# Attention biases with the window masks already in them: shifted tables of 46 rows, border rows loaded in three pieces

## The reference

```python
def row_block(r):
    rs = jnp.clip(r - kr // 2, 0, rows - kr)
    q_r = lax.dynamic_index_in_dim(q, r, axis=1, keepdims=False)
    k_r = lax.dynamic_slice_in_dim(k, rs, kr, axis=1)[:, :, col_idx]
    v_r = lax.dynamic_slice_in_dim(v, rs, kr, axis=1)[:, :, col_idx]
    dr = rs + jnp.arange(kr) - r + (NA_ROW_WIN - 1)
    bias = rpb32[:, dr[None, :, None], dc[:, None, :]]
    sc = jnp.einsum('bqhd,brqwhd->bhqrw', q_r, k_r).astype(jnp.float32) + bias[None]
    p = jax.nn.softmax(sc.reshape(b, NA_HEADS, GRID_W, kr * NA_COL_WIN), axis=-1)
    p = p.reshape(b, NA_HEADS, GRID_W, kr, NA_COL_WIN).astype(v.dtype)
    return jnp.einsum('bhqrw,brqwhd->bqhd', p, v_r)
```

## Time and profile before

| what | us |
|---|---|
| median of 3 runs | 2937.93 |
| lowest and highest run | 2933.5, 2955.96 |
| the profiled execution | 2952.27 |
| its span | 2950.5 |
| TensorE busy in the span | 2737.9 (93%) |
| VectorE busy | 1404.5 (48%) |
| ScalarE busy | 886.3 (30%) |
| POOL busy | 877.5 (30%) |
| input stage | 0 to 655 |
| Fourier stage | 655 to 795 |
| attention | 795 to 1131 |
| mixer output | 1131 to 1520 |
| feed-forward | 1520 to 2950 |

### The profile page before, as it was taken

How to read it: one execution, slowest core, us unless ns; L and a number is a source line. 1 busy time by engine, 2 the same in 40 slices (tenths; PEclk the granted TensorE clock), 3 DMA queues, 4 the chain that set the end, 5 groups by cost and what they waited for, 6 DMA issues and landing times. The chain is left out here.

```text
span 2950.5 us, 33892 instructions
## 1 busy us (share of the span) xinstructions
PE 2737.9 (93%) x12792; PEld 2274.7 (77%) x12792; DVE 1404.5 (48%) x2280; ACT 886.3 (30%) x1595; POOL 877.5 (30%) x491
## 2 busy tenths in 40 slices
PE   7999999998768896999985999997999999999997
PEld 5888888877657785777774888885888888888886
DVE  4300000006458785544336999998565554122232
ACT  3311111112345551211224444443222223343332
POOL 1010011103222224333204666664000004555553
PEclk9999999999879997999997999998999999999999
DMA  4322144426565645555535777776666665564653
GB/s 140 97 93 72 55 133 152 148 96 220 168 155 149 162 125 165 179 186 169 174 107 208 278 280 278 275 285 221 223 221 221 222 221 193 178 204 139 206 175 111
DMA packets 235537, 522.34 MB, mean 177 GB/s; under 512 B 47732, under 2 KB 73200, under 8 KB 231664
## 3 DMA queue, kind: packets, MB, share of 16 engines
q1 hardware_dynamic: 214128, 499.21, 51.3%
q10 hardware_dynamic: 21248, 20.97, 2.1%
HBM read 336.55 MB, written 185.10 MB: 177 GB/s over the span
## 5 line engine op out<-in xcount | busy, mean ns | idle before, releaser
L2205 PE MATMUL ff_psum<-ff_w,ff_hid 128*128 128x512 f32 x2112 | 479.3, 389 | 1.3 <-POOL ff_w L1798 1.3
L2205 PEld LDWEIGHTS ff_psum<-ff_w,ff_hid 128*128 128x128 f32 x2112 | 396.4, 188 | 84.1 <-POOL ff_w L1798 1.7
L1798 POOL TENSOR_TENSOR ff_w<-ff_st,ff_w 128x512 fp32r<-128x512 f32 x176 | 249.5, 1425 | 634.0 <-ACT ff_w L2041 633.6
L1798 POOL TENSOR_TENSOR ff_w<-ff_wraw,ff_w 128x512 fp32r<-128x512 f32 x154 | 269.1, 1749 | 240.9 <-ACT ff_w L2041 240.9
L422 PE MATMUL in_psum<-in_hA,in_w 128*128 128x512 f32 x1440 | 327.9, 389 | 0.0
L422 PEld LDWEIGHTS in_psum<-in_hA,in_w 128*128 128x128 f32 x1440 | 270.4, 188 | 56.0
L2166 PE MATMUL ff_psum<-ff_h,ff_w 128*128 128x512 f32 x1056 | 247.4, 393 | 27.2 <-DVE ff_h L1864 27.2
L2166 PEld LDWEIGHTS ff_psum<-ff_h,ff_w 128*128 128x128 f32 x1056 | 200.5, 190 | 70.6 <-POOL ff_w L1798 28.6
L2166 PE MATMUL ff_psum<-ff_h,ff_again 128*128 128x512 f32 x1056 | 244.7, 391 | 4.0 <-DVE ff_h L1864 4.0
L2166 PEld LDWEIGHTS ff_psum<-ff_h,ff_again 128*128 128x128 f32 x1056 | 199.3, 189 | 45.9 <-issue 4.4
L1464 PE MATMUL mo_psum<-mo_act,mo_w 128*128 128x512 f32 x768 | 191.8, 407 | 33.8 <-POOL mo_act L1315 21.0
(11 more groups left out here) (181 smaller groups left out, 4031.2 us busy)
## 6 DMA issues: line engine op xcount, KB each, us to landing
split<-ff_w SPq DMA_DIRECT2D x154, 512.0 KB, 3.6
ff_again<-split SPq DMA_DIRECT2D x154, 512.0 KB, 4.1
ff_st<-in_w_down_dram SPq DMA_DIRECT2D x176, 256.0 KB, 2.9
ff_wraw<-in_w_up_dram SPq DMA_DIRECT2D x44, 512.0 KB, 5.7
hidden<-ff_c SPq DMA_DIRECT2D x44, 512.0 KB, 3.0
ff_kraw<-hidden SPq DMA_DIRECT2D x44, 512.0 KB, 4.3
at_bias<-shifted SPq DMA_DIRECT2D x72, 256.0 KB
in_raw<-in_w_in_dram SPq DMA_DIRECT2D x32, 512.0 KB, 5.0
```

The lines of the kernel that those rows point to most:

```text
L1798: nc.gpsimd.tensor_tensor(split_out(i, 1), parts(i), f32(split_out(i, 0)), ALU.subtract).then_inc(w_tail, 1)
L2205: last = nc.tensor.matmul(ps[:, 4 * (1 - half) + t], hid[:, a, (b * PAIRS + pair) % 2, q, t * P:(t + 1) * P], weights(i)[:, e], start=(r = ...
```

## The change

Masks are no longer added on chip. They are put into the tables in memory:

- `padded` becomes two tables of 46 rows, filled with -1e30 from a host array. One holds only the 16 columns of offsets that an inner query's window has, the other all 31. Each holds, below one another, a copy with the 8 row offsets of an inner window (the first 31 rows) and one with all 15 (the 15 rows from `NEAR_R`). Four inserts of `rpb` parts for one.
- `shift` goes over 63 pieces for 48: a border query column takes one part of its 32 columns from the full table and the rest from the other. A table has 46 rows for 31, so a shift of full width has 8 x 46 runs of 128 bytes for 8 x 31. They are dealt out evenly over the 48 gate tiles.
- `load_bias` takes row kind 0 and row kind 2 (three column kinds each) in three pieces: one of 3 query rows with 16 key rows (2 KB runs), and for the 5 other query rows two of 8 key rows (1 KB runs). Row kind 1 is loaded as before. That is 21 loads a head for 9, of the same bytes.
- `window`, `sides`, POOL's nine additions, the load of the side masks and VectorE's 72 additions go.
- The reduction waits for the loads of its own row kind (`bias_in[h % 2][i]`) and no more for an addition; the very first tile waits for its own three loads.

```diff
-REL_R, REL_C = 31, 64
+NEAR_R, REL_R, REL_C = 31, 46, 64
+FULL_C = ((0, COL_WIN // 2, 0), (0, 0, 0), (COL_WIN // 2 + 1, QC, COL_WIN))
+SHIFTS = [piece for j in range(KINDS) for c in range(QC)
+          for piece in (((j, c, 0, 0, KC),) if not FULL_C[j][0] <= c < FULL_C[j][1] else
+                        ((j, c, 1, FULL_C[j][2], COL_WIN), (j, c, 0, COL_WIN - FULL_C[j][2], COL_WIN)))]
+ROW_PIECES = (
+    ((0, 3, 0, KR, BASE_R[0] - (QR - 1)), (3, QR, ROW_WIN, KR, BASE_R[0] - (QR - 1)), (3, QR, 0, ROW_WIN, NEAR_R)),
+    ((0, QR, 0, KR, BASE_R[1] - (QR - 1)),),
+    ((3, QR, 0, KR, BASE_R[2] - (QR - 1)), (0, 3, 0, ROW_WIN, BASE_R[2] - (QR - 1)), (0, 3, ROW_WIN, KR, NEAR_R - ROW_WIN)),
+)
...
             def shift(n):
-                j, c = divmod(n, QC)
-                sp.dma_start(shifted[j, :, c], padded[:, :, BASE_C[j] - c:BASE_C[j] - c + KC]
+                j, c, full, k, run = SHIFTS[n]
+                at = BASE_C[j] - c + k
+                sp.dma_start(shifted[j, :, c, :, k:k + run], padded[full, :, :, at:at + run]).then_inc(padded_in, 16)
...
-            sp.wait_ge(zero_done, 1)
+            sp.dma_start(padded.rearrange("f h r c -> (f h r c)").rearrange("(p y) -> p y", p=P), mask).then_inc(padded_in, 16)
...
-                    sp.dma_start(padded[:, PAD_R:PAD_R + RPB_R, PAD_C:PAD_C + RPB_C], rpb).then_inc(padded_in, 16)
+                    for full_c in range(2):
+                        for full_r in range(2):
+                            insert(full_c, full_r)
...
                 for b in range(GB):
-                    shift(GB * t + b)
+                    shifts(GB * t + b)
...
             def load_bias(h, i):
                 for j in range(KINDS):
                     rows = shifted[j, h]
-                    src = bass.AP(rows.tensor, rows.offset + (BASE_R[i] - (QR - 1)) * KC,
-                                  [[KC, QR], [REL_R * KC, QC], [1, KR * KC]])
-                    sp.dma_start(bias[:, h % 2, i * KINDS + j], src).then_inc(
-                        first_in if h == i == 0 else bias_in[h % 2], 16)
+                    for r0, r1, k0, k1, base in ROW_PIECES[i]:
+                        src = bass.AP(rows.tensor, rows.offset + (base + r0 + k0) * KC,
+                                      [[KC, r1 - r0], [REL_R * KC, QC], [1, (k1 - k0) * KC]])
+                        sp.dma_start(bias[r0 * QC:r1 * QC, h % 2, i * KINDS + j, k0 * KC:k1 * KC], src
+                                     ).then_inc(first_in if h == i == j == 0 else bias_in[h % 2][i], 16)
...
-                dve.wait_ge(bias_ready, h * NB + kind + 1)
+                if n == 0:
+                    dve.wait_ge(first_in, 16 * len(ROW_PIECES[0]))
+                else:
+                    loads = KINDS * len(ROW_PIECES[KIND[i]]) * (h // 2 + 1)
+                    if h % 2 == 0 and KIND[i] == 0:
+                        loads -= len(ROW_PIECES[0])
+                    dve.wait_ge(bias_in[h % 2][KIND[i]], 16 * loads)
...
-                b = bias[:, h % 2, kind]
-                V.tensor_tensor(b, b, window[:, kind], ALU.add).then_inc(bias_ready, 1)
```

More of the change, by code:

```diff
@@ L101, with input_phase @@
 RPB_R, RPB_C = 2 * ROW_WIN - 1, 2 * COL_WIN - 1
+FULL_C = ((0, COL_WIN // 2, 0), (0, 0, 0), (COL_WIN // 2 + 1, QC, COL_WIN))
[7 more added lines that the diff above has]
+)
 NEG = -1.0e30
-def input_phase(nc, const_in, step, steps, low, raw, x, w_in, norm_g, b_gate, eye, rpb, u_out, qT_out, v_out, kT_out, gT_out, gate_w,
+def input_phase(nc, const_in, step, steps, low, raw, x, w_in, norm_g, b_gate, eye, rpb, mask, u_out, qT_out, v_out, kT_out, gT_out, gate_w,
                 padded, shifted):
@@ L249, in shift, with insert, shifts @@
             def shift(n):
-                j, c = divmod(n, QC)
-                sp.dma_start(shifted[j, :, c], padded[:, :, BASE_C[j] - c:BASE_C[j] - c + KC]
-                             ).then_inc(padded_in, 16)
-            sp.wait_ge(zero_done, 1)
-            sp.dma_start(padded.rearrange("h r (x c) -> (h r x) c", x=1).rearrange("(p y) c -> p (y c)", y=2),
-                         zero).then_inc(padded_in, 16)
+                j, c, full, k, run = SHIFTS[n]
+                at = BASE_C[j] - c + k
+                sp.dma_start(shifted[j, :, c, :, k:k + run], padded[full, :, :, at:at + run]).then_inc(padded_in, 16)
+            def insert(full_c, full_r):
+                c, nc_ = (0, RPB_C) if full_c else (COL_WIN - 1 - COL_WIN // 2, COL_WIN)
+                r, nr = (0, RPB_R) if full_r else (ROW_WIN - 1 - ROW_WIN // 2, ROW_WIN)
+                at = NEAR_R if full_r else PAD_R + r
+                sp.dma_start(padded[full_c, :, at:at + nr, PAD_C + c:PAD_C + c + nc_], rpb[:, r:r + nr, c:c + nc_]
+                             ).then_inc(padded_in, 16)
+            def shifts(m):
+                slots = NG * GB
+                for i in range(m * len(SHIFTS) // slots, (m + 1) * len(SHIFTS) // slots):
+                    shift(i)
+            sp.dma_start(padded.rearrange("f h r c -> (f h r c)").rearrange("(p y) -> p y", p=P), mask).then_inc(padded_in, 16)
             for q in range(4):
@@ L839, in window_mask, with attention_phase @@
 def window_mask():
[L841 to L858, removed]
+    return np.full((P, 2 * HEADS * REL_R * REL_C // P), NEG, np.float32)
+def attention_phase(nc, const_in, low, raw, qk_in, qT, kT, v, shifted, eye, atT_out):
     KT = KR * KC // P
@@ L887, in attention_phase @@
         ps = m.banks()
-        v_in, bias_in = m.sems("v_in", 2), m.sems("bias_in", 2)
-        sides_in, window_done = m.sem("sides_in"), m.sem("window_done")
+        v_in, bias_in = m.sems("v_in", 2), [m.sems(f"bias_in{i}_", KINDS) for i in range(2)]
         first_in = m.sem("first_in")
-        qk_heads, q_tail, k_tail, bias_ready = (m.sem(x) for x in ("qk_heads", "q_tail", "k_tail", "bias_ready"))
+        qk_heads, q_tail, k_tail = (m.sem(x) for x in ("qk_heads", "q_tail", "k_tail"))
         s_mm, s_red, p_exp, pT_mm, pT_copied, o_mm, inverted, o_done = (
@@ L914, in _ @@
         def _(sp):
-            sp.dma_start(sides[:, 0:KINDS * (KR + KC)], mask).then_inc(sides_in, 16)
             sp.dma_start(ident[:, :], eye).then_inc(const_in, 16)
@@ L972, in _ @@
             G = nc.gpsimd
[L974 to L980, removed]
             up = slice(HEAD_DIM, P)
-            pool.wait_ge(sides_in, 16)
-            window_kind(0, 0)
             for rows, heads in ((slice(0, QR), 3), (slice(QR, ROWS), 2 * PARTS)):
                 pool.wait_ge(qk_heads, heads)
-                pool.wait_ge(window_done, 1 if heads == 3 else KINDS)
+                if heads > 3:
+                    pool.wait_ge(q_tail, 1)
                 G.tensor_tensor(qs[up, 0, rows], qraw[up, rows], f32(qs[up, 0, rows]), ALU.subtract).then_inc(q_tail, 1)
[L989 to L992, removed]
             pool.wait_ge(q_tail, whole(0))
-            for i in range(1, KINDS):
-                for j in range(KINDS):
-                    window_kind(i, j)
             for h in range(1, HEADS):
@@ L2244, in encoder_layer @@
             raw = Pool(nc, ctx, "in").sb("raw", [P, 2 * SEQ])
-            input_phase(nc, const_in, step, steps, low, raw, x, w_in, norm1_g, b_gate, eye, rpb, u, qT, v, kT, gT,
+            input_phase(nc, const_in, step, steps, low, raw, x, w_in, norm1_g, b_gate, eye, rpb, mask, u, qT, v, kT, gT,
                         gate_w, padded, shifted)
             fourier_phase(nc, step, steps, low, raw, qk_in, qT, kT, u, pos_table, chan_table, fnT, gate_w, b_gate, gT)
-            attention_phase(nc, const_in, low, raw, qk_in, qT, kT, v, shifted, mask, eye, atT)
+            attention_phase(nc, const_in, low, raw, qk_in, qT, kT, v, shifted, eye, atT)
         mixer_output_phase(nc, const_in, step, steps, x, fnT, atT, gT, w_mix, w_out, norm2_g, eye, x2, hT)
```

17 lines of the change are left out of this document (4 added, 13 removed).

## The result

The changed kernel takes 2993.2 us in the median of its runs (2990.4 to 3012.8), the kernel before 2941.3 beside it: a ratio of 1.0185, with a 95% interval from 1.0125 to 1.0244, so 52 us more. The forecast was 2998 us (+60) in a range of 2963 to 3030. The profiled execution took 2993.8 us with a span of 2992.0, for 2952.3 and 2950.5 before.

The account below looks back on a forecast made before the run. The prediction took attention to be bound by four DMA engines carrying values besides bias, q and k. Added packets +63 us and the last sum -3 gave +60, 2998 us against the median, range 2963 to 3030.

Parts of the forecast that it names:

- The narrow engines: Attention: the four DMA engines that carry values as well as bias, q and k set the pace, 33.1 to 37.5 us a head.
- A load runs on as many engines as its source has outer steps: Attention's loads: 3-row pieces use three engines and 5-row pieces five, always the lowest; main case, chance 0.75.
- The two rivals with 8 or 16 engines: Border pieces spread over eight engines (2935 us, chance 0.08) or all sixteen (2908 us, chance 0.05).
- The added packets: Border bias loads: 192 more 1 KB packets a head on each of three engines, 9.0 us a head, +63 us.
- step by step price: Expectation for border kinds in two 4-row pieces: 96 more 2 KB packets a head at 0.085 us, 8.2 us a head.
- the 1 KB term: Border bias loads: 1 KB packets at 0.047 us each (bounds 0.042 to 0.058), 63 us in all (57 to 77).
- The contention: Attention's q and k packets might run cheaper with three engines trailing alone: 35 us back, taken as nothing, kept for the range.
- The sums: VectorE's 72 bias and mask additions: six stretched ones beside POOL's k_tail hidden, only the seventh on the path, 3.1 us gained.
- if the cover were gone: Attention: were the stretched additions not hidden by ScalarE's wait for DMA, removing all seven would give 22 us.
- Dead time per load: Rival: each small bias load costs its engines up to 0.57 us besides packets, +48 us, 3046 us; chance 0.12.
- Costs at nothing: SP's 25 issues a head, DVE's waits per row kind, the extra input-stage shifts and the last values: 0 us each.
- What would show it: Signs: 168 L925 issues, DMA share 3/16 to 5/16, k_tails 45 to 48 us apart, ScalarE's wait over 100 us, VectorE 76 us less.

Follow-up runs that it names:

- the halves: The kernel before, masks added on chip, with each border kind loaded in two pieces of 4 query rows, all 2 KB packets: 3000.1 us, ratio 1.0193.
- Kernels with the engine load of the kernel before: The changed kernel with border kinds loaded whole (2948.3 us), and the kernel before with border loads cut along the run, 21 a head (2943.8 us).
- whole loads: The changed kernel with every row kind loaded whole, 9 bias loads a head, border tiles getting wrong masks: 2948.3 us, ratio 1.0022.
- the two kernels without cover: Changed kernel and kernel before, each with bias and values on 16 engines and a second raw buffer for q and k: 2894.0 and 2916.1 us.

## Why the prediction came out right, and where it did not

**The bound: right.** The narrow engines set the stage. Removing four-engine value loads gave 25 and 62 us, removing a serial wait in front of q and k gave nothing.

**A load runs on as many engines as its source has outer steps: right at 3 and 5 as well.** The forecast had read 4, 8 and 16 from rows. The means over pieces and values (26.6 and 26.0%) would also fit four engines for every piece, and so would the added time, 9.0 us a head by the same prices. The windows of 1 us decide: 19.0% and 30.9%, three engines and five, beside 26.2% for the halves. The Trainium skill's rule, the largest number up to 16 that divides the slowest dimension of both sides (page "DMA: Bandwidth & Descriptors", section "Why a DMA increments its semaphore by 16 and not by 1") agrees with each of them. The two rivals with 8 or 16 engines fell.

**The added packets: right in mechanism, a little too dear.** Price times number was 192 x 0.047 = 9.0 us a head, 63 in seven. A packet of 1 KB measures 0.047 us where it runs. But the stream grew by 6.5 us a head in the changed kernel (45.4 / 7; 0.034 a packet) and by 7.9 in the kernel with pieces alone (55.3 / 7; 0.041). Halves with 2 KB packets grew it by 7.9 for 8.2. These are differences of single executions, and the one before took 11 us more than the median of its runs, while the changed kernel's stood at its median. Kernels with the engine load of the kernel before had streams of 38.4 and 36.9 us a head for its 37.8, in executions of 2954.3 and 2945.4 us. The medians are the better measure: +51.9 us for the changed kernel, and 3.1 more that the end of the stage gave back (below), are 55 us, 7.9 a head; the pieces alone +56.8, 8.1 a head; the halves +57.0, 8.1 for the 8.2 of the step by step price. So the 2 KB term holds, and the 1 KB term was some 10% too large as a cost of the stage, although the packet itself was priced right. Where that last 1 us a head goes stays open. The contention that I had left at nothing (35 us to come back) is not it: I looked for a relief on the bias packets, and the halves, which should have had it too, show none.

**The sums: six hidden, and the seventh's 3 us are there.** From the last landing of q and k to the mixer's first issue are 66.8 to 68.8 us in the five kernels without sums in which ScalarE waits in every head, and 70.3 to 70.8 in the four with sums that wait in head 7: 3.1 us less on average, the 3.1 of the prediction. The medians are too coarse for it. The whole removal measures 6 us more with whole loads (ratio interval 1.0004 to 1.0040) and 2 us less with pieces (1.0192 to 1.0185, within the intervals). The other end of that bound was 22 us "if the cover were gone": between the two kernels without cover it measures 2916.1 - 2894.0 = 22.1 us. That the figures meet so closely is in part luck. The prediction took 3.1 us for each of the seven, which is right for the four of 3.8 us; the three of 4.7 us are 4.05 above a plain one, so the seven are 24.5 us in all. And the two kernels differ in the other ways named above. In the kernel with sums and without cover the stretching is still there:

```profile
905.70 4.74 DVE L1054 TENSOR_TENSOR at_bias<-at_bias,at_window 128x512 f32<-128x512 f32 x1
```

In the changed kernel no VectorE instruction beside POOL is stretched; its reductions last 671 to 693 ns in all 128.

**Dead time per load: refuted.** 12 more loads a head cost 0 (0.9982 to 1.0017) where up to 48 us were thought possible.

**Costs at nothing: held.** SP's issues, the waits per row kind, the shifts, and the last values: no wait for values stands in head 7. One wait that I had not foreseen came and cost nothing: the values of heads 1 to 6 are late by 5 to 9 us now (TensorE's wait at L1126, as the one at 877.45), but they fall into the stretch in which ScalarE stands for q and k anyway (885.22 in that head).

```profile
877.45 1.94 PE L1126 MATMUL at_psum<-at_vs,at_pT 128*128 128x64 f32 x8 [6.77 <-issue]
...
885.22 0.63 ACT L1046 ACTIVATE in_low<-in_raw 128x512 fp32r<-128x512 f32 x1 [14.46 <-DMA in_raw<-kT]
```

**What would show it:** 168 issues, a share near 4/16, ScalarE's wait over 100 us (116.3) and unchanged stages came as written. The k_tails are 43.7 us apart for the 45 to 48 expected, the same shortfall as above. VectorE's busy time fell by 59 and not by 76 us: attention's fell by 64, since busy time counts what overlaps once and the sums overlapped their neighbours, and the other stages came out 5 us longer in this execution.

**The sum.** +52 us in the medians for +60: the added packets made some 55 us of their 63, and the 3 us of the last sum came off that as forecast. The mis-sized term is that of the 1 KB packets. The 35 us of contention and the dead time, which made the range wide, both came to nothing.

## What to carry to other kernels

Count for each DMA engine, not for the sum of them: a stage can stand still on four engines while the mean share is half. Ahead of any edit to a load, read how many outer steps its source will have, since a cut that leaves fewer steps puts the same bytes on fewer engines (57 us here), while a cut along the run cost nothing here. Work taken off an engine that is not the bound moves into the next wait; take the bound away first (here by spreading loads and issuing q and k earlier), and a difference of 22 us appears.

## What the hardware showed that I had not expected

- Twice the engines gave 11% more bandwidth: loads of 16 partitions each on 16 engines moved 165 GB/s at 0.21 us for a 2 KB packet, for 148 GB/s at 0.115 us with loads of 128 partitions on eight.
- Small packets were free where eight engines shared them: border kinds in runs of 1 KB and 512 bytes for 2 KB, 2943.8 us for 2942.6.
- A load of 3 query rows runs on three engines, 19.0% of 16, and one of 5 on five, 30.9%.
- A transfer's wait can change its owner without any change in time: 116.3 us of ScalarE waiting for q and k became 22.4, TensorE waited for values instead, and the median went from 2993.2 to 2994.6 us.
